# Who sums the squares of the first MLP's input norm: TensorE chunk by chunk, or GpSimd with one sum over partitions

## What is computed

```python
def rmsnorm(x, g):
    xf = x.astype(jnp.float32)
    y = xf * lax.rsqrt(jnp.mean(xf * xf, axis=-1, keepdims=True) + RMS_EPS)
    return (y * g.astype(jnp.float32)).astype(x.dtype)

x = x + rmsnorm(mix @ w_out[l], norm_mix_post[l])
h = rmsnorm(x, norm_mlp_pre[l])
u = jnp.square(jax.nn.relu(h @ w_mlp_up[l]))
x = x + rmsnorm(u @ w_mlp_down[l], norm_mlp_post[l])
```

## Time and profile before

| | |
|---|---|
| median of 3 runs | 2907.81 us (2905.55 to 2909.16) |
| profiled execution: its time | 2911.12 us |
| its span, first to last instruction | 2909.0 us |
| mean granted TensorE clock | 0.987 of full |
| TensorE matmul busy | 2807.1 us, 96% |
| VectorE, ScalarE, GpSimd busy | 1969.2, 1331.1, 102.6 us |

### The profile page before, as it was taken

The page is one execution under the profiler, slowest core; times in us unless marked ns, Lnnn a source line. Parts: engine busy times, 40 slices in busy tenths (PEclk is TensorE's granted clock), DMA queues, the critical chain, the costliest instruction groups (busy, mean ns, idle before and its releaser), DMA issues.

```text
span 2909.0 us, 51387 instructions
## 1 busy us (share of the span) xinstructions
PE 2807.1 (96%) x16426; PEld 2434.7 (84%) x16426; DVE 1969.2 (68%) x3243; ACT 1331.1 (46%) x2155; POOL 102.6 (4%) x188
## 2 busy tenths in 40 slices
PE   5999999999999999999999899999889999999997
PEld 4888888888887888888888698788778888888886
DVE  6778877766657764567744645755578885688855
ACT  4565555554444443334443444544454443444443
POOL 0000000000010000000000000000010000000000
PEclk9999999999999999999999899999999999999999
DMA  4544544445553556666655344343355545555554
GB/s 153 174 167 171 196 162 145 155 173 177 192 186 116 187 192 220 206 204 209 211 188 192 142 159 156 105 164 118 116 166 187 187 174 191 196 187 188 181 174 152
DMA packets 87098, 503.29 MB, mean 173 GB/s; under 512 B 10213, under 2 KB 18693, under 8 KB 35803
## 3 DMA queue, kind: packets, MB, share of 16 engines
q1 hardware_dynamic: 83468, 491.05, 48.0%
q0 software_dynamic: 2992, 10.86, 1.4%
q10 hardware_dynamic: 576, 0.58, 0.1%
HBM read 500.29 MB, written 10.55 MB: 176 GB/s over the span
## 4 chain that ended last, share of the span: by engine, by line
PE 82%; DVE 7%; issue 5%; ACT 3%; DMA 1%; DVEq 1%; ACTq 0%; SPq 0%
PE PS L536 47%; PE PS L542 24%; ACT w L998 2%; DVE w L1542 1%; DVE tmp L1553 1%; PE PS L618 1%; PE PS L619 1%; PE PS L620 1%; PE PS L553 1%; PE PS L797 1%; PE PS L789 1%; DMA w_raw<-in_w_OB 1%; PE PS L555 1%; PE PS L554 1%; PE PS L641 0%
## 5 line engine op out<-in xcount | busy, mean ns | idle before, releaser
L1542 DVE TENSOR_TENSOR w<-w_raw,w 128x1024 fp32r<-128x1024 f32 (+3 forms) x1020 | 1102.7, 1117 | 412.6 <-ACT w L998 409.3
L998 ACT ACTIVATE w<-w_raw 128x1024 fp32r<-128x1024 f32 (+3 forms) x1020 | 946.9, 965 | 422.1 <-PE PS L542 240.4
L536 PE MATMUL PS<-h,w 128*128 128x512 f32 x3104 | 809.0, 401 | 17.2 <-DVE h L1576 10.9
L536 PEld LDWEIGHTS PS<-h,w 128*128 128x128 f32 x3104 | 562.3, 190 | 152.7 <-issue 29.2
L542 PEld LDWEIGHTS PS<-h,w 128*128 128x128 f32 x3104 | 426.4, 191 | 31.2
L536 PE MATMUL PS<-u,w 128*128 128x512 f32 x1728 | 440.8, 393 | 5.4 <-ACT w L998 5.4
L542 PE MATMUL PS<-h,w 128*128 128x256 f32 x3104 | 435.3, 283 | 0.0
L536 PEld LDWEIGHTS PS<-u,w 128*128 128x128 f32 x1728 | 308.1, 189 | 58.6 <-ACT w L998 6.0
L536 PE MATMUL PS<-f,w 128*128 128x512 f32 x1408 | 353.1, 392 | 2.7 <-issue 2.6
L536 PEld LDWEIGHTS PS<-f,w 128*128 128x128 f32 x1408 | 253.3, 189 | 48.5 <-issue 2.8
L542 PEld LDWEIGHTS PS<-u,w 128*128 128x128 f32 x1728 | 241.0, 190 | 20.9
(11 more groups left out here) (269 smaller groups left out, 2510.0 us busy)
## 6 DMA issues: line engine op xcount, KB each, us to landing
w_raw<-in_w_FU SPq DMA_DIRECT2D x88, 1024.0 KB, 4.8
w_raw<-in_w_UP SPq DMA_DIRECT2D x64, 1024.0 KB, 4.8
w_raw<-in_w_DN SPq DMA_DIRECT2D x64, 1024.0 KB, 4.7
w_raw<-in_w_FD SPq DMA_DIRECT2D x64, 704.0 KB, 4.1
w_raw<-in_w_G SPq DMA_DIRECT2D x32, 1024.0 KB, 4.7
w_raw<-in_w_Q SPq DMA_DIRECT2D x18, 1024.0 KB, 4.7
w_raw<-in_w_X SPq DMA_DIRECT2D x16, 1024.0 KB, 4.8
w_raw<-in_w_Y SPq DMA_DIRECT2D x16, 1024.0 KB, 4.8
```

The source lines that it names most:

```text
L536: pe.matmul(PS[:, bank, :], w_hi[:, 2 * s + hf, k * P:(k + 1) * P], rhs[:, k0 + k].rearrange("p a b -> p (a b)"), start=start and k == 0, ...
L998: act.activation(w_hi[:, 2 * s + hf, 0:n * P], w_raw[:, s, off * P:(off + n) * P], ACT.Copy)\
L1542: tt(w_lo[:, slot, 0:n * P], w_raw[:, s, off * P:(off + n) * P], w_hi[:, slot, 0:n * P].bitcast(F32), ALU.subtract).then_inc(lo_ready, 1)
```

## The change

Norm 2 goes over to GpSimd's way. GpSimd calls `add_squares` for norms 1, 2 and 3 and not for norm 4. In `product`, the first unit of `UP0` no longer has ones-matmuls between its chunks; behind it comes `sum_features(2)` with its two ones-matmuls. Norm 4 stays with TensorE.

```diff
             for norm in range(1, 5):
-                if norm % 2:
+                if norm < 4:
                     add_squares(norm)
                 else:
                     free_last_square(norm)
...
-            def half_unit(u, s, hf, n, bank, rhs, k0, start, stop, ready=None, wide=True, norm=None):
+            def half_unit(u, s, hf, n, bank, rhs, k0, start, stop, ready=None, wide=True):
...
                         pe.matmul(PS[:, bank, :], w_hi[:, 2 * s + hf, k * P:(k + 1) * P],
                                   rhs[:, k0 + k].rearrange("p a b -> p (a b)"), start=start and k == 0, stop=False)
-                        if norm is not None:
-                            add_square(norm, k0 + k)
...
                         follow = ready if isinstance(i, int) and s == 0 else None
-                        norm_here = norm if follow and norm == 2 else None
-                        half_unit(u, s, 0, n0, s, rhs, 0, True, False, follow, wide, norm_here)
+                        half_unit(u, s, 0, n0, s, rhs, 0, True, False, follow, wide)
                         if mid is not None:
                             mid(i, s)
-                        half_unit(u, s, 1, n1, s, rhs, n0, False, True, follow, wide, norm_here)
-                        if norm == 5 and follow:
+                        half_unit(u, s, 1, n1, s, rhs, n0, False, True, follow, wide)
+                        if norm is not None and follow:
                             sum_features(norm)
```

## The result

| | before | changed |
|---|---|---|
| median of 20 runs each | 2909.73 us (2905.55 to 2913.12) | 2914.16 us (2910.48 to 2917.94) |
| profiled execution: span | 2909.0 us | 2911.1 us |
| VectorE busy | 1969.2 us | 1975.1 us |
| GpSimd busy | 102.6 us | 116.0 us |
| TensorE matmul busy | 2807.1 us | 2800.7 us |

The ratio of changed to before is 1.0014, with a 95% interval of 1.0008 to 1.0021: 2.3 to 6.1 us slower, 4.1 us at its centre (the two medians lie 4.4 us apart). The forecast was +4.0 us, as 2911.8 us in the range 2907.0 to 2916.0 us; 2914.2 us were measured, and 2 us of the distance are the median of before, which rose from 2907.81 us (3 runs) to 2909.73 us (20 runs). The forecast said that a change of this size can't be told from none; with 20 runs of each kernel it can, since the interval lies above 1. TensorE lost 6 us of work and the kernel became slower.

The account below looks back on a forecast made before the run. In norm 2 VectorE's chunks, not TensorE, were taken as the bound. Terms -3.8 + 6.5 - 0.5 = +2.2 us, plus 1.8 us for the tail, gave +4.0 us: 2911.8 us, range 2907.0 to 2916.0 us.

Parts of the forecast that it names:

- The bound: Norm 2: TensorE follows VectorE's chunks; from 930 us TensorE is always busy, so a shift of UP0 shifts the end.
- Part 1: Norm 2's chunk loop: without the 16 ones-matmuls VectorE runs at its own pace, gaining 3.8 us.
- the ring: Norm 2's chunk loop: TensorE's ones-matmul, ScalarE's high part, VectorE's gain_lo, TensorE; costs 4.1 us over 15 steps.
- Part 2: Norm 2's chunks: GpSimd's 13 adds cost VectorE 0.48 us each, plus 0.3 us copy: 6.5 us, less 0.5 us.
- such pairs: GpSimd operations beside VectorE operations reading two SBUF tiles, seen at 2148.54 us (0.48 us lost) and 1680.57 us (1.03 us).
- Rival 2: Loop of add_branch: each add holds VectorE its whole 0.74 us; +7.4 us, slower by over 0.2%; chance 0.22.
- Part 3: From the last gain_lo to unit 2 of UP0: sums now come last, at half clock; +1.8 us (0 to +2.5).
- T+10.0 and T+10.15: T is the last gain_lo's start; unit 2 of UP0 expected at T+10.0 by ScalarE's weights; TensorE's unit 1 starts T+4.4, takes 5.75 us.
- half clock all through norm 2: TensorE, fed one L536 per about 1.6 us without ones-matmuls, was expected to stay at half clock.
- sign (d): Profile after: granted clock 0.5 from 874 us until after the last chunk, first unit's 8 L542 in 1.9 us.
- Rival 3: TensorE's clock comes back before the end of norm 2's stage: only 2.2 us remain, 2910.0 us; chance 0.13.
- The sum: Whole kernel: 2.2 us at the last gain_lo plus 1.8 us behind it, +4.0 us, 2911.8 us.

Follow-up runs that it names:

- no_adds: Changed kernel without GpSimd's adds of squares 1 to 14 in norm 2, the copy kept: 2907.54 us, ratio to before 0.9997.
- the third profile: The changed kernel profiled once more with no edit, a single execution: 2913.55 us.
- half_adds: Changed kernel with GpSimd's adds of norm 2 over 128 of the 256 tokens only: 2912.06 us, ratio to before 1.0007.

## Why the prediction was right, point by point

**The bound.** Right. VectorE's chunks and not TensorE set the stage, what TensorE lost in work came to nothing, and the stretch behind the stage gave nothing back.

**Part 1, the ring is cut.** Right in mechanism, a little small in size. I put VectorE's own pace at 1.14 us and the gain at 3.8 us. Without adds the chunks take 17.0 us against 21.2: 4.2 us. The 0.3 us given back for ScalarE's last steps was too much. That cutting the ring is worth this by itself is shown by the two kernels that cut it on TensorE, 16.9 us. The prediction spread the ring's cost evenly over 15 steps, though, and that isn't how it lies. Two `gain_lo` of the kernel before that waited for the ring at half clock:

```profile
876.61 0.48 DVE L1597 SCALAR_TENSOR_TENSOR h<-x,par,h  x1 [1.51 <-ACT h L1037]
...
879.93 0.48 DVE L1597 SCALAR_TENSOR_TENSOR h<-x,par,h  x1 [0.71 <-ACT h L1037]
```

The four steps up to 879.93 us took 7.2 us where 1.14 us each would be 4.6, and the eleven behind took 14.0 us for 12.5. So 2.6 us of the ring's cost fell into the short stretch at half clock, and 1.5 us into the rest, where the pace isn't even either but goes between 1.1 and 1.5 us.

**Part 2, the adds.** Right in mechanism, and the value taken was good. I took 0.48 us per add from one row of the same size and got 0.46 us per step of the loop. 13 adds and the copy were put at 6.5 us less 0.5, so 6.0; measured are 22.7 - 17.0 = 5.7 us for the adds and 0.13 us for the copy, which `no_adds` still has (`scaled` beside it takes 0.61 us) and which I had put at 0.3. For parts 1 and 2 together I wrote +2.2 us; in the first profiles of the two kernels it is +1.5 us, against the mean of both profiles of before +1.7 us. The prediction says that such pairs stand at two places of the trace; there are more, between 2117 and 2141 us, and they would have given the same price (`gain_lo` 1.00 us at 2117.82 us).

**Rival 2** (0.74 us per add, slower by over 0.2%) fell. An add of 0.74 us cost VectorE 0.46 us, so for about 0.3 us of the duration that the profile gives it, GpSimd's add doesn't hold VectorE. Which part of the add that is, at its start or its end, no run shows.

**Part 3, the tail.** The order of events came as written: root behind the ones-matmuls, reciprocal 4.7 us behind the last `gain_lo` (I wrote 5.1), 8 matmuls L540 in 1.91 us. The distance of 0.87 us from one ones-matmul to the next at half clock, which the prediction only estimated, is 0.85 us in the third profile (896.81 to 897.66). The two paths to unit 2, ScalarE's weights and TensorE's own unit 1, end together, as the prediction had them (T+10.0 and T+10.15). I took +1.8 us; four profiles give +1.2, +1.4, +1.8 and +1.6. The step "half clock all through norm 2" holds in three of them; in the first the clock was up for some 3 us in the middle, behind the 8 L540 back to back (884.49 to 886.40 us), and fell again, against sign (d) of the prediction:

```profile
886.00:888.00 2.00, 1.62 (x4) 0.60 (x3) 2.00 (x5) 0.81 (x2) 1.38 (x2) 0.56 0.00 0
888.00:890.00 2.00, 0.50 (x1) 0.19 (x1) 2.00 (x4) 1.18 (x3) 1.33 (x2) 1.00 0.03 8
890.00:892.00 2.00, 0.60 (x2) 0.29 (x2) 2.00 (x5) 1.22 (x4) 0.96 (x1) 0.80 0.00 0
892.00:894.00 2.00, 1.20 (x2) 0.47 (x2) 2.00 (x5) 0.85 (x3) 1.25 (x2) 0.50 0.00 0
```

It was down again before the tail, so it brought nothing. The same happened in `no_adds` and `half_adds` (up at about 884.5 and 885 us, down again by 889 us). Rival 3 had the clock back in time for the tail; it wasn't.

**The sum.** +4.0 us predicted, +4.1 us measured, but the stage itself is worth 3.2. So the hit to 0.1 us is in part luck: the working is 0.8 us too large in the stage, 0.5 us in the chunks (+2.2 against 22.7 less 20.95, the mean of the two profiles of before) and 0.3 us in the tail (+1.8 against +1.5, the mean of four).

## What to carry to other kernels

Before an element-wise step goes over to GpSimd, look at what VectorE does at the same time: if both read two tiles of SBUF, the step costs VectorE most of the step's own duration (0.46 of 0.74 us for 128x256 here), and taking work off an engine that had been waiting anyway (TensorE here) gained nothing against it. A ring in which an engine waits for a tile to be freed is cut more cheaply by more tiles, or by writing into a tile that has just died (the chunks fell from 21.2 and 20.7 us to 16.9, and no cost showed elsewhere). And matmuls that wait for another engine can be worth their place for the clock alone: ask what runs behind them at half speed if they go.

## What the runs showed that I had not expected

TensorE with two matmuls more per chunk finished the stage earlier, 31.8 against 32.2 to 32.9 us, and without GpSimd's adds 25.8 against 27.6 us. The same instruction stream had its clock rise anywhere between the first and the end of the second ones-matmul of the tail, which moved the tail by up to 0.7 us from profile to profile. And GpSimd's adds and VectorE's `gain_lo` locked into a fixed phase: 12 of the 16 `gain_lo` of the first profile took 0.94 us or a little more while `scaled` and `add` mostly kept theirs, so that reading L1594 alone one would take a slow `gain_lo` for the trouble, where it only stands behind GpSimd.
